# Held accumulations in four half-tile passes, with the squares summed by halves

## The reference

```python
def rms_norm(x, g):
    xf = x.astype(jnp.float32)
    y = xf * lax.rsqrt(jnp.mean(xf * xf, axis=-1, keepdims=True) + EPS)
    return (y * g.astype(jnp.float32)).astype(x.dtype)
...
    x = x + rms_norm(h @ w_out, norm_post)      # h: what the half block computed
    h = next_part(rms_norm(x, norm_pre))
```

## Time and profile before

| what | us |
|---|---|
| median of three runs | 1155.91 (1153.86 to 1158.71) |
| the profiled execution | 1155.11 |
| its span, first to last instruction | 1153.3 |
| PE busy, with 7268 matmuls | 1093.7 (95%) |
| DVE busy | 811.7 (70%) |
| ACT busy | 615.1 (53%) |

### The profile page before, as it was taken

One profiled execution on the slowest core, in us unless ns is written; L12 is line 12 of the kernel. 1 busy time (PEld: TensorE's weight loads), 2 busy tenths in 40 slices (PEclk: granted clock), 3 DMA queues, 4 the chain that ended last, 5 costly groups with the idle time before them and its releaser, 6 DMA issues.

```text
span 1153.3 us, 20642 instructions
## 1 busy us (share of the span) xinstructions
PE 1093.7 (95%) x7268; PEld 988.7 (86%) x7268; DVE 811.7 (70%) x1271; ACT 615.1 (53%) x1060; POOL 126.1 (11%) x139
## 2 busy tenths in 40 slices
PE   7999999999999999989999998999788898999997
PEld 7878999999789997779999997998676687999996
DVE  6757777776744667877777777688978557666664
ACT  6657444444846747656444446465338746444442
POOL 0230111111010012201111110000412200000000
PEclk9999999999999999999999999899899999999999
DMA  8254555554554654425555652445001263655540
GB/s 335 91 188 165 201 192 191 194 189 163 209 180 161 199 178 157 158 92 193 191 199 183 199 185 90 165 162 179 7 1 36 93 220 120 206 183 189 190 148 37
DMA packets 51381, 185.08 MB, mean 160 GB/s; under 512 B 5728, under 2 KB 6240, under 8 KB 51328
## 3 DMA queue, kind: packets, MB, share of 16 engines
q1 hardware_dynamic: 49248, 178.28, 45.3%
q0 software_dynamic: 1504, 5.44, 1.3%
q10 hardware_dynamic: 576, 0.64, 0.2%
HBM read 183.28 MB, written 1.05 MB: 160 GB/s over the span
## 4 chain that ended last, share of the span: by engine, by line
PE 84%; DVE 10%; ACT 3%; issue 2%; DMA 0%; DVEq 0%; SPq 0%; ACTq 0%
PE ps L208 26%; PE ps L166 18%; PE ps L167 17%; PE ps L168 17%; DVE w_lo L149 2%; DVE arena L1523 2%; PE ps L678 1%; DVE x L403 1%; DVE a_lo L385 1%; DVE arena L396 1%; PE ps L707 1%; PE ps L1405 1%; PE ps L691 1%; PE ps L944 1%; ACT a_hi L379 0%
## 5 line engine op out<-in xcount | busy, mean ns | idle before, releaser
L149 DVE TENSOR_TENSOR w_lo<-raw,w_hi 128x1024 fp32r<-128x1024 f32 x336 | 419.3, 1257 | 143.0 <-ACT w_hi L144 143.0
L144 ACT ACTIVATE w_hi<-raw 128x1024 fp32r<-128x1024 f32 x336 | 347.3, 1054 | 167.0 <-PE ps L168 102.2
L166 PE MATMUL ps<-a_hi,w_hi 128*128 128x256 f32 x1408 | 401.6, 285 | 2.6 <-DVE a_lo L385 2.2
L167 PE MATMUL ps<-a_lo,w_hi 128*128 128x256 f32 x1408 | 399.7, 284 | 0.0
L168 PE MATMUL ps<-a_hi,w_lo 128*128 128x256 f32 x1408 | 399.6, 284 | 0.0
L166 PEld LDWEIGHTS ps<-a_hi,w_hi 128*128 128x128 f32 x1408 | 271.2, 193 | 6.7 <-issue 3.0
L167 PEld LDWEIGHTS ps<-a_lo,w_hi 128*128 128x128 f32 x1408 | 271.3, 193 | 2.5
L168 PEld LDWEIGHTS ps<-a_hi,w_lo 128*128 128x128 f32 x1408 | 271.3, 193 | 0.0
L208 PE MATMUL ps<-w_hi,a_hi 128*128 128x512 f32 x496 | 158.5, 401 | 9.3 <-DVE a_lo L1149 3.0
L208 PE MATMUL ps<-w_lo,a_hi 128*128 128x512 f32 x496 | 154.0, 391 | 0.0
L208 PE MATMUL ps<-w_hi,a_lo 128*128 128x512 f32 x496 | 153.8, 391 | 0.0
(11 more groups left out here) (187 smaller groups left out, 1081.5 us busy)
## 6 DMA issues: line engine op xcount, KB each, us to landing
raw<-in_w SPq DMA_DIRECT2D x336, 512.0 KB, 3.9
row<-in_rows POOLq DMA_DIRECT2D x7, 512.0 KB, 4.0
x<-in_x SPq DMA_DIRECT2D x2, 512.0 KB, 4.2
out<-x SPq DMA_DIRECT2D x4, 256.0 KB, 2.0
misc<-in_misc POOLq DMA_DIRECT2D x1, 512.0 KB, 5.7
arena<-in_ws POOLq DMA_DIRECT2D x1, 512.0 KB, 7.3
tab<-in_tables POOLq DMA_DIRECT2D x1, 320.0 KB, 4.4
tab<-in_tables POOLq DMA_DIRECT2D x1, 256.0 KB, 5.0
```

The lines of the kernel that those rows point to most:

```text
L144: act.activation(w_hi[:, s, :], raw[:, s, :], ACT.Copy).then_inc(hi_done, 1)
L149: dve.tensor_tensor(w_lo[:, s, :], raw[:, s, :], w_hi[:, s, :].bitcast(F32), ALU.subtract).then_inc(lo_done, 1)
L166: pe.matmul(o, l_hi, r_hi, start=first, stop=False)
L167: pe.matmul(o, l_hi, r_lo, start=False, stop=False)
```

## The change

`held_pe` now makes four passes over the four held units: tile 0 left half, tile 0 right half, tile 1 left, tile 1 right. A pass is 12 matmuls, three for each unit. After each of the first three a signal `part` is given. The transposes of tile 0 stand after the first unit of the fourth pass.

The square is taken by halves (`square_act`). DVE turns the first half's sum into sum/1024 + EPS (`base`), and the root of the second half's sum takes that as its bias (`root_act`), so that the two sums are never added by an instruction of their own. The product with the gain row moves into `term_dve`, a half at a time, and `add_dve` keeps the reciprocal and the two additions. A few waits count to four sums where they counted to two.

```diff
-        for n, slot in held:
-            ready(slot)
-            mm = accumulate(pe, n, slot, first and n == held[0][0], n == u.n_last, tiles=(0,))
-        mm.then_inc(u.tile0, 1)
-        for n, slot in held[:-1]:
-            accumulate(pe, n, slot, first and n == held[0][0], False, tiles=(1,))
-        if turn_early:
-            turn_tile_pe(pe, u, 0, x)
-        n, slot = held[-1]
-        accumulate(pe, n, slot, False, True, tiles=(1,))
+        for tt, c in ((0, 0), (0, 1), (1, 0), (1, 1)):
+            for n, slot in held:
+                if tt == 0 and c == 0:
+                    ready(slot)
+                mm = accumulate(pe, n, slot, False, n == u.n_last, tiles=(tt,), cs=(c,))
+                if turn_early and tt and c and n == held[0][0]:
+                    turn_tile_pe(pe, u, 0, x)
+            if not (tt and c):
+                mm.then_inc(u.part, 1)
...
-    def post_act(act, u, tt):
-        acc_ready(act, u, tt)
-        act.activation(junk[:, :], acc[tt], ACT.Square,
-                       accum_out=st[:, tt:tt + 1]).then_inc(u.sum, 1)
-        act.wait_ge(u.sum, TT * u.n + tt + 1)
-        act.activation(st[:, 4 + tt:5 + tt], st[:, tt:tt + 1], ACT.Sqrt, bias=EPS_COL,
+    def square_act(act, u, tt, h):
+        acc_ready(act, u, tt, h)
+        act.activation(junk[:, half(h)], acc[tt][:, half(h)], ACT.Square,
+                       accum_out=st[:, 20 + 2 * tt + h:21 + 2 * tt + h]).then_inc(u.sum, 1)
+
+    def root_act(act, u, tt):
+        act.wait_ge(u.base, TT * u.n + tt + 1)
+        act.wait_ge(u.sum, 4 * u.n + 2 * tt + 2)
+        act.activation(st[:, 4 + tt:5 + tt], st[:, 21 + 2 * tt:22 + 2 * tt], ACT.Sqrt, bias=st[:, 24 + tt:25 + tt],
                        scale=1.0 / D).then_inc(u.root, 1)
...
+    def term_dve(dve, u, tt, h, r):
+
+        acc_ready(dve, u, tt, h)
+        dve.wait_ge(u.sum, 4 * u.n + 2 * tt + h + 1)
+        if h == 0:
+            dve.tensor_scalar(st[:, 24 + tt:25 + tt], st[:, 20 + 2 * tt:21 + 2 * tt], 1.0 / D, EPS,
+                              ALU.mult, ALU.add).then_inc(u.base, 1)
+            if tt == 0:
+                dve.wait_ge(row_loaded[r % 2], 16 * (r // 2 + 1))
+        dve.tensor_tensor(ybuf[:, tt, half(h)], acc[tt][:, half(h)], row[:, r % 2, half(h)],
+                          ALU.mult).then_inc(u.term, 1)
+
+    def add_dve(dve, u, tt):
+
+        dve.wait_ge(u.root, TT * u.n + tt + 1)
+        dve.reciprocal(st[:, 6 + tt:7 + tt], st[:, 4 + tt:5 + tt]).then_inc(u.inv, 1)
+        dve.wait_ge(u.inv, TT * u.n + tt + 1)
+        dve.wait_ge(u.term, 4 * u.n + 2 * tt + 2)
         for h in range(2):
...
     def update_act(act, u, g, following, early):
 
         act.preload_act_table(ACT.Sqrt)
-        post_act(act, u, 0)
+        square_act(act, u, 0, 0)
+        square_act(act, u, 0, 1)
+        root_act(act, u, 0)
+        square_act(act, u, 1, 0)
         hi_tile_act(act, u, 0, g)
-        post_act(act, u, 1)
+        square_act(act, u, 1, 1)
+        root_act(act, u, 1)
...
     def update_dve(dve, u, g, r, early, rows=None):
-        add_dve(dve, u, 0, r)
+        term_dve(dve, u, 0, 0, r)
+        term_dve(dve, u, 0, 1, r)
+        add_dve(dve, u, 0)
+        term_dve(dve, u, 1, 0, r)
         lo_tile_dve(dve, u, 0, g)
-        add_dve(dve, u, 1, r)
+        term_dve(dve, u, 1, 1, r)
+        add_dve(dve, u, 1)
```

More of the change, by code:

```diff
@@ L196, in tokens, with accumulate @@
             mm.then_inc(unit_used, 1)
-    def accumulate(pe, n, slot, first, last, i=0, tiles=range(TT)):
+    def accumulate(pe, n, slot, first, last, i=0, tiles=range(TT), cs=range(2)):
         s = n % RING
-        if tiles[0] == 0:
+        if tiles[0] == 0 and cs[0] == 0:
             pe.wait_ge(lo_done, n + 1 + RING * i)
@@ L206, in accumulate @@
                                (a_lo, w_hi, False, last)):
-                for c in range(2):
+                for c in cs:
                     mm = pe.matmul(ps[:, 2 * tt + c, :], a[:, slot, t],
                                    b[:, s, c * 512:(c + 1) * 512], start=f, stop=z)
-        if tiles[-1] == TT - 1:
+        if tiles[-1] == TT - 1 and cs[-1] == 1:
             mm.then_inc(unit_used, 1)
@@ L214, in build @@
     pre_sems = signals("pre", "sum mean root inv scaled turned hi lo")
-    post_sems = signals("post", "tile0 term sum root inv added")
+    post_sems = signals("post", "part base term sum root inv added")
     next_sems = signals("next", "sum root inv scaled turned hi lo row row_out")
@@ L219, in build @@
     Pre = namedtuple("Pre", "lo base")
-    Update = namedtuple("Update", "n n_last tile0 term sum root inv added next")
+    Update = namedtuple("Update", "n n_last part base term sum root inv added next")
     ROW = cut(16384, SEQ)
@@ L300, in build, with acc_ready @@
     acc = [ps[:, 2 * tt:2 * tt + 2, :].rearrange("p a b -> p (a b)") for tt in range(TT)]
-    def acc_ready(eng, u, tt):
-        if tt:
+    def acc_ready(eng, u, tt, h):
+        if tt and h:
             eng.wait_ge(unit_used, u.n_last + 1)
         else:
-            eng.wait_ge(u.tile0, u.n + 1)
+            eng.wait_ge(u.part, 3 * u.n + 2 * tt + h + 1)
     def after(u):
@@ L459, in scaled_update_act @@
         act.preload_act_table(ACT.Sqrt)
-        post_act(act, u, 0)
+        for h in range(2):
+            square_act(act, u, 0, h)
+        root_act(act, u, 0)
         next_act(act, u, 0)
-        post_act(act, u, 1)
+        for h in range(2):
+            square_act(act, u, 1, h)
+        root_act(act, u, 1)
         hi_tile_act(act, u, 0, g, range(4))
@@ L470, in scaled_update_dve @@
     def scaled_update_dve(dve, u, g, r):
[L471 to L474, removed]
+        for tt in range(TT):
+            for h in range(2):
+                term_dve(dve, u, tt, h, r)
+            add_dve(dve, u, tt)
+            scale_tile_dve(dve, u, tt)
         lo_tile_dve(dve, u, 0, g)
@@ L481, in last_update_act @@
         for tt in range(TT):
-            post_act(act, u, tt)
+            for h in range(2):
+                square_act(act, u, tt, h)
+            root_act(act, u, tt)
     def last_update_dve(dve, u, r):
         for tt in range(TT):
-            add_dve(dve, u, tt, r)
+            for h in range(2):
+                term_dve(dve, u, tt, h, r)
+            add_dve(dve, u, tt)
     F_CV, F_GL, F_PR, F_GR = cut(3072, 2, SEQ), cut(3584, 2, SEQ), cut(4096, 2, SEQ), cut(4608, 2, SEQ)
@@ L534, in ffn_pe @@
         held = [(f_out(n0, t), f_slot(t)) for t in range(FT - HELD, FT)]
-        held_pe(pe, following, held, lambda slot: pe.wait_ge(f.lo, FT - HELD + [s for _, s in held].index(slot) + 1),
-                False, turn_early)
+        held_pe(pe, following, held, lambda slot: pe.wait_ge(f.lo, FT - HELD + [s for _, s in held].index(slot) + 1), turn_early)
     def ffn_act_step(act, f, n0, t, i, split):
@@ L1000, in held_ready @@
             pe.wait_ge(g_sem.lo, j + 1)
-        held_pe(pe, updates[2], [(N_SGO + j, s_slot(j)) for j in range(SGT - HELD, SGT)], held_ready, False, True)
+        held_pe(pe, updates[2], [(N_SGO + j, s_slot(j)) for j in range(SGT - HELD, SGT)], held_ready, True)
     def s_slot(j):
@@ L1596, in attn2_pe @@
         pe.wait_ge(at2.lo, KT // 2)
-        held_pe(pe, updates[4], [(N_WO2 + k, k) for k in range(2 * KT - HELD, 2 * KT)], lambda slot: None, False, True)
+        held_pe(pe, updates[4], [(N_WO2 + k, k) for k in range(2 * KT - HELD, 2 * KT)], lambda slot: None, True)
     def attn2_act(act):
@@ L1698, in mlp_pe @@
         held_pe(pe, following, held,
-                lambda slot: pe.wait_ge(m_sem.lo, MT - HELD + [s for _, s in held].index(slot) + 1), False, False)
+                lambda slot: pe.wait_ge(m_sem.lo, MT - HELD + [s for _, s in held].index(slot) + 1), False)
     def mlp_act(act):
```

20 lines of the change are left out of this document (4 added, 16 removed).

## The result

The changed kernel takes 1159.85 us (median of 20 runs, 1155.86 to 1165.0), the kernel before 1155.93 (20 runs on the same chip). The ratio is 1.0033, 95% interval 1.0021 to 1.0044: a loss of 3.9 us, where 2.75 was forecast. It lies inside the range and under the 0.5% that the prediction took as the least that can be told from no change; with 20 runs of each kernel the interval excludes no change all the same. The profiled execution took 1156.39, its span 1154.6, so it is one of the shorter ones, and the trace is read for places, not for the last microsecond. One execution each of experiments 5 and 10 and two of the kernel before beside them took 1539 to 5531 us; medians and ratios here are without them.

The account below looks back on a forecast made before the run. The prediction took PE as the bound, busy 1093.7 of 1153.3 us. Earlier waits of 7.2 less a tail gain of 4.45 gave +2.75 on 1155.11, 1157.9, plus 0.8 for the median: 1158.7 us, range 1153.8 to 1163.9.

Parts of the forecast that it names:

- The matmuls themselves: Held parts on PE: 48 matmuls before and after, three in a row into one PSUM bank cost nothing, 0.
- Earlier waits: Held parts' first pass: units wanted every 3 matmuls instead of 6, so PE stalls for operands; loss 7.2 us, bounds 5.2 to 8.
- The tail: ACT and DVE work ending each update: shorter square, earlier products and transposes; gain 4.45 us, bounds 2.5 to 6.4.
- The price of the half square: ACT's square at an update's end: 512 columns take 0.60 against 1.02 for 1024, 0.42 us less.
- The sum: Whole kernel: 7.2 lost less 4.45 gained, +2.75 us on the profiled execution.
- rival 3: Update ends: each of six gains its full 1.1 us, 6.4 in all; +0.8, giving 1156.7 us; 15%.
- Rival 1: Held-part stalls in both FFNs also lower the granted clock, 5.1 us more, giving 1163.8 us; 17%.
- a low clock in a window where it was 1.00: Changed profile's windows: the prediction's stated sign of being wrong, besides a first pass without gaps; no size given.
- dense work on both sides of the stall: Case against a clock fall at held-part stalls: a mixer wait of 2.26 us between dense work left the window at 1.00.
- rival 2: Behind the fourth update: the clock fall goes away as the tail gets denser by 0.85 us; 5.1 us less, 1153.6; 13%.
- 4: First held pass: all operands ready, no stalls, only the gain left, giving 1151.5 us; 2%.

Follow-up runs that it names:

- experiment 5: New operations, both tiles unit by unit, tile 0's hi and lo pieces ahead of tile 1's left square and product; 1157.23 us, ratio 1.0015 to the kernel before.
- 10: experiment 1 with one small product in place of four in the second group keeping PE busy at update ends; 1149.99 us, ratio 0.9949 to the kernel before.
- Experiment 3: Kernel before with half-tile passes over tile 1 only, old operations, transposes still 18 matmuls behind tile 0; 1155.18 us, ratio 0.9994.
- experiment 1: Changed kernel with tile 0's held units added unit by unit again, only the last half by half; 1150.38 us, ratio 0.9959 to the kernel before.
- experiment 2: Changed kernel's four passes with the old ACT and DVE operations, transposes 18 matmuls behind tile 0; 1163.54 us, ratio 1.0069 to the kernel before.
- experiment 7: experiment 1 with one square of the whole tile, behind the left product, in place of two half squares; 1158.19 us, ratio 1.0017 to the kernel before.
- experiment 8: Changed kernel with small products in PE's stalls, seven in both FFNs and one in the SGU; 1159.61 us, ratio 1.0039 to the kernel before.
- experiment 9: experiment 1 with seven small products behind tile 1's transposes of the fourth update; 1148.66 us, ratio 0.9941 to the kernel before.
- experiments 4: New operations with both tiles unit by unit, each last unit left half then right, transposes behind tile 1's third unit; 1164.78 us, ratio 1.0083 to the kernel before.
- experiments 6: experiment 1 with the row products back in `add_dve`, each right ahead of its addition; 1155.36 us, ratio 0.9994 to the kernel before.

## Why the prediction was right, step by step
- **The matmuls themselves, 0:** right. Experiment 3 puts passes over tile 1 at 0.9994 (0.9981 to 1.0007), and PE's busy time is 1092.6 after 1093.7.
- **Earlier waits, 7.2 (bounds 5.2 to 8):** the mechanism is the forecast's, stall by stall: the fourth unit in U1 and U3, the third and fourth in U0, the second and third in U2, none in U4. The trace gives 1.83 in U0 and 2.06 in U1 for 1.8 and 2.05, and without the two falls 1.1 in U2, 2.25 in U3 and 0.1 in U5 for 1.2, 2.05 and 0.1: 7.4 in all. In U3 the last operand is ready 4.24 us behind the held part's start, where it was 3.95; why is not shown. By time the passes over tile 0 cost 8.7 and 8.8 us (two pairs of kernels; the intervals leave about 2 us either way on the better pair, changed against 1), so 7.2 is not contradicted, but both pairs lie above it. The falls of the clock inside the held parts, 3.4 us in the profiles of the changed kernel and of experiment 2 alike, are not in the 7.2.
- **The tail, 4.45 (bounds 2.5 to 6.4):** 4.2 by two pairs. By the trace 0.69 in U0 and U2 and 0.68 in U4 for 0.65, 0.94 in U3 for 0.85, and 1.16 at the end for 1.0. In U1, where the next half block's first matmuls overlap the held ones, the time from the last held matmul to the first matmul behind tile 1's transposes goes from 4.92 to 4.13, 0.79 for 0.65. That is 4.95 in all. The price of the half square, 0.42, is exact for its own row (1.02 to 0.60). In U0 the explanation was wrong in its main part, and that the size came out (0.69 for 0.65) is partly luck. I put the 0.65 down to the earlier transposes, and held that a shorter square alone would bring nothing. With the earlier transposes and a whole square, experiment 7, the gap is 4.80, only 0.13 under the 4.93 before; the half square gives the other 0.57. The earlier transposes may still be a condition: with half squares, transposes 18 matmuls behind and the pieces first, experiment 5 has 5.50, but there both squares of tile 1 stand behind the pieces as well, so it is not a test of the transposes alone. The next half block's first operand hangs on the last square by way of the small products that keep PE busy until the second inverse root. The chain of waits in U0 of the changed kernel shows it, where the earlier trace rows has DVE's lo pieces:
```profile
98.66 0.70 ACT arena L362 x2
99.40 2.05 PE ps L238 x16
101.45 0.23 PE ps L344 x2
```
- **The sum, +2.75:** measured +3.9 (2.4 to 5.1), so 2.75 is inside the interval. By time the earlier waits are the term that came out larger, 8.7 for 7.2, but within the noise of the pairs. A small slip in the bounds: six updates at 1.1 are 6.6, and rival 3 has 6.4.
- **Rival 1, the stall costs the clock too:** its sign was seen, 0.50 inside two held parts where it had been 1.00, and its price was not. The prediction also named this, a low clock in a window where it was 1.00, as a way of being wrong, so by its own last sentence it failed in that point: the time came out, the clock's part of the picture did not. The forecast's case against it, dense work on both sides of the stall, does not hold: U3's stall has that and the clock falls behind it. In U1 it doesn't here, and in the profile of experiment 2 it does, behind the same stall of 1.77 us (0.50 at 288:290). But each fall cost 1.7 us and not 5.1, and in the same execution the one behind U3 got 3.4 smaller, which is a part of rival 2. Over the runs the mean granted clock is 0.984 for both kernels, so nothing shows that the 3.9 us went to the clock. The Trainium skill ("TensorE: Matmul & The Clock Gate", section "HAM oscillation — how this bites in real kernels") blames idle gaps of PE for such falls, with waits in its example that are longer than the stalls here. These runs bear it out only in part: with U3's stall cut from 2.06 to 0.55 us (experiment 8) there is no fall, but U2's wait of 1.36 us is followed by one in the changed kernel and by none in experiments 2 and 8, and behind U3 the fall stays when the gap ahead of it goes from 2.15 to 0.59 (experiment 9).
- **Rivals 2, 3 and 4:** 2 names U3's denser tail as the reason for a smaller fall, and that isn't it: experiment 8 has the same 8.93 us behind U3's held part and loses 5.1 again. 3 is out, with U0's gain at 0.69 and not 1.1; 4 is out by the stalls.

What stays open is the clock. Experiment 1 runs at a mean of 0.986, the kernel before at 0.984, and between runs of one kernel 0.001 of clock goes with 0.75 us (all runs together); so, as an estimate from these means, some 1.5 of its 5 us may be smaller falls. Which ones, and why they are smaller, no run tells.

## What to carry to other kernels
Splitting an accumulation so that a part of the sums is done early shortens the tail, but it also asks for every operand in the first pass. Before reordering, put the time at which each operand is ready beside the time at which the new order wants it; split only the passes in which everything is there (here tile 1, which kept the whole gain, 5 us). And an instruction that is moved ahead in a queue to use an early result holds up what stood there if that result comes late: experiments 4 and 5 differ by 7.9 us through the order in two queues alone. Last, a gap measured from one event says nothing of what was lost ahead of it: experiments 6 and 7 lose a part of their time inside the held part.

## What the runs showed of the hardware
- A square of 128x512 sums with its total shows 0.60 us on ACT and 0.19 to read the total, against 1.02 for 128x1024 with a read of 0.19 to 0.26. The two rows overlap: from the square's start to the end of the read it is 0.68 for a half (98.66 to 99.34 in the changed kernel) and 1.11 for a whole (1146.72 to 1147.83 before). Two halves back to back take 1.27 (90.42 to 91.69 in experiment 6), 0.16 more than one whole.
- Matmuls of 128x512 keep 0.23 us each at the full clock whether they alternate between two PSUM banks or fill one, and take 0.43 at the low level (705.89 to 708.45 in the changed kernel, six in 2.56 us).
- In all profiles here a fall of the granted clock loses about 1.7, 3.4 or 5.1 us in one place, and a stall of 1.4 to 2.1 us of PE between dense matmuls is sometimes followed by one (U2 and U3 of the changed kernel, U1 and U3 of experiment 2) and sometimes not (U0 and U1 of the changed kernel, U0 and U2 of experiment 2, U2 of experiment 8). Summed over a whole execution up to the last matmul, the profiles lose from 10.3 us (experiment 1; 12.0 the second time, and in 9 and 10) to 18.8 (2).
